# A trunk layer with retrieved experts: gathered rows issued in step with TensorE's tiles, and two one-hot buffers in the first half

## The reference, cut to what matters

```
act = gelu(einsum('nd,ned->ne', hx, expert_u[ix]))      # 128 picks of each token
return einsum('ne,ned->nd', act * gx, expert_v[ix])     # weighted sum of 128 rows of expert_v
```

## Time and profile before

| | us |
|---|---|
| median of 3 runs | 5171.36 (5170.26 to 5171.77) |
| the profiled execution, whole | 5173.29 |
| its span, first to last instruction | 5171.4 |

### The profile page before, as it was taken

One profiled execution on the slowest core, in us unless ns is written; L12 is line 12 of the kernel. 1 busy time (PEld: TensorE's weight loads), 2 busy tenths in 40 slices (PEclk: granted clock), 3 DMA queues, 4 the chain that ended last, 5 costly groups with the idle time before them and its releaser, 6 DMA issues.

```text
span 5171.4 us, 54598 instructions
## 1 busy us (share of the span) xinstructions
PE 4792.5 (93%) x22501; PEld 3572.5 (69%) x22501; DVE 3023.1 (58%) x4381; ACT 578.9 (11%) x1078; POOL 1701.1 (33%) x1113
## 2 busy tenths in 40 slices
PE   5989999998999999999999899999988899998869
PEld 1786446447998444466555346999988899997768
DVE  1441017886766765347777579666665517766671
ACT  1521001421222000000000011100000000000000
POOL 0131002663654655202544344223322203333220
PEclk7999999998999999999999999999999999999989
DMA  9919989993224989987999885688899959999994
GB/s 393 377 43 357 322 321 363 375 406 144 85 70 161 387 338 378 401 336 294 420 420 420 358 326 211 253 323 319 337 417 417 406 204 367 380 375 406 415 412 156
DMA packets 262299, 1666.66 MB, mean 322 GB/s; under 512 B 28274, under 2 KB 32770, under 8 KB 78660
## 3 DMA queue, kind: packets, MB, share of 16 engines
q0 software_dynamic: 130048, 939.72, 45.6%
q1 hardware_dynamic: 123460, 673.84, 33.9%
q10 hardware_dynamic: 8544, 49.62, 2.4%
HBM read 1643.31 MB, written 18.94 MB: 321 GB/s over the span
## 4 chain that ended last, share of the span: by engine, by line
PE 30%; DMA 18%; DVE 6%; issue 1%; POOL 0%; ACT 0%; ACTq 0%; DVEq 0%
PE ps L241 16%; DMA arena_sb<-peer_v 11%; PE ps L2289 8%; DMA arena_sb<-peer_u,arena_sb 6%; PE ps L1720 4%; PE ps L2232 2%; DVE arena_sb L400 1%; DVE arena_sb L395 1%; DMA arena_sb<-peer_v,arena_sb 1%; DVE arena_sb L2477 1%; POOL arena_sb L349 0%; DVE arena_sb L2002 0%; DVE arena_sb L2012 0%; DVE arena_sb L2004 0%; DVE arena_sb L1821 0%
## 5 line engine op out<-in xcount | busy, mean ns | idle before, releaser
L241 PE MATMUL ps<-arena_sb 128*128 128x224 f32 (+3 forms) x9728 | 2312.7, 399 | 5.0 <-PEq L552 2.4
L241 PEld LDWEIGHTS ps<-arena_sb 128*128 128x128 f32 x9728 | 1688.3, 193 | 623.4 <-issue 335.8
L400 DVE SCALAR_TENSOR_TENSOR arena_sb<-arena_sb 128x2048 f32<-128x2048 f32 x412 | 987.1, 2396 | 318.4 <-DMA arena_sb<-peer_v,arena_sb 301.4
L395 DVE CUSTOM_DVE_ANT_0 arena_sb<-arena_sb 128x2048 f32<-128x2048 f32 x416 | 961.7, 2332 | 222.3 <-DMA arena_sb<-peer_u,arena_sb 221.9
L349 POOL DMA_INDIRECT arena_sb<-peer_v,arena_sb x416 | 646.8, 1555 | 1071.0 <-DVE arena_sb L400 960.0
L2289 PE MATMUL ps<-arena_sb 128*128 128x224 f32 x4096 | 832.8, 364 | 141.2 <-DMA arena_sb<-peer_v 140.5
L349 POOL DMA_INDIRECT arena_sb<-peer_u,arena_sb x416 | 628.0, 1510 | 998.3 <-DVE arena_sb L395 792.4
L2289 PEld LDWEIGHTS ps<-arena_sb 128*128 128x128 f32 x4096 | 792.8, 196 | 179.7 <-DMA arena_sb<-peer_v 171.5
L1570 PE MATMUL ps<-arena_sb 128*128 128x512 f32 x768 | 342.2, 603 | 20.6 <-PEq L2594 7.4
L1720 PE MATMUL ps<-arena_sb 128*128 128x512 f32 x640 | 278.7, 598 | 17.0 <-DVE arena_sb L1501 13.5
L1570 PEld LDWEIGHTS ps<-arena_sb 128*128 128x128 f32 x768 | 145.8, 193 | 212.4 <-issue 194.9
(11 more groups left out here) (279 smaller groups left out, 2984.4 us busy)
## 6 DMA issues: line engine op xcount, KB each, us to landing
arena_sb<-peer_ut SPq DMA_DIRECT2D x128, 1024.0 KB, 8.3
arena_sb<-peer_v SPq DMA_DIRECT2D x128, 1024.0 KB, 15.3
arena_sb<-w_mod POOLq DMA_DIRECT2D x64, 1024.0 KB, 9.1
arena_sb<-w_qkv SPq DMA_DIRECT2D x48, 1024.0 KB, 8.7
arena_sb<-w_out SPq DMA_DIRECT2D x48, 1024.0 KB, 8.0
arena_sb<-w_query SPq DMA_DIRECT2D x48, 1024.0 KB, 6.9
arena_sb<-w_mod SPq DMA_DIRECT2D x32, 1024.0 KB, 8.9
arena_sb<-w_ga_r SPq DMA_DIRECT2D x32, 1024.0 KB, 7.7
```

The costliest lines, as they stand in the source:

```text
L241: mm = pe.matmul(out, weights[:, k * P:(k + 1) * P], x[:, k, :], start=(k == 0), stop=(k == chunks - 1))
L395: nc.vector.tensor_tensor_reduce(rows, rows, total, 1.0, 0.0, ALU.mult, ALU.add, seg.dots[:, p:p + 1]).then_inc(t.rows_used, 1)
L400: nc.vector.scalar_tensor_tensor(out=total, in0=rows, scalar=seg.weight[:, p:p + 1], in1=total, op0=ALU.mult, op1=ALU.add).then_inc(t.rows ...
```

## The change

`counts` is a new list of 253 entries, 375 rows in all. POOL goes through `behind` and, before it issues the rows of an entry k > 1 that has any, waits until `tile` is at least k - 1; the wait for the free slot stays. In h = 0 the one-hot operands get a second buffer, in memory that is otherwise used by `kept` from the V tiles on; group g uses buffer g % 2, `hot` of group g waits only for `gates` of group g - 2, and stands on DVE after the rows of tile s - 2 in place of s - 1 (groups 0 and 1 both after tile 11). In h = 1 there is one buffer and `hot` stands after the rows of tile s - 1, as before.

```
-    counts = ([0] * 10 + [2, 1] * 27 + [1, 2, 1, 2, 1, 1, 2, 1] * 8 + [2, 1] * 32 + [2] * 60)
+    counts = [0] * 8 + [2, 2, 2, 1] * 14 + [1, 2, 1, 1, 2] * 12 + [1, 2, 1, 1] + [2, 1, 2, 2] * 16 + [1] + [1, 2, 1, 1] * 15

     def _(pool):
-        gather_until(pool, nc, t, a, lead.stop)
-        pool.wait_ge(spare_in, 16 * 11)
-        gather_until(pool, nc, t, a, spare.stop)
-        pool.wait_ge(t.index_done, 1)
-        gather_until(pool, nc, t, a, last.stop)
+        for k, rows in enumerate(behind):
+            if k > 1 and len(rows):
+                pool.wait_ge(tile, k - 1)
+            for seg, known, n in ((spare, spare_in, 16 * 11), (last, t.index_done, 1)):
+                if seg.start in rows:
+                    gather_until(pool, nc, t, a, seg.start)
+                    pool.wait_ge(known, n)
+            gather_until(pool, nc, t, a, rows.stop)

-    weighted = ring[3][:, 0:TOKENS * P].rearrange("p (u n) -> p u n", u=TOKENS)
-    plain = ring[3][:, TOKENS * P:TOKENS * (P + HALF)].rearrange("p (u n) -> p u n", u=TOKENS)
+    hots = ring[3], t.m[:, C + 8192:C + 8192 + TILE]
+    weighted = [ap[:, 0:TOKENS * P].rearrange("p (u n) -> p u n", u=TOKENS) for ap in hots]
+    plain = [ap[:, TOKENS * P:TOKENS * (P + HALF)].rearrange("p (u n) -> p u n", u=TOKENS) for ap in hots]

+    hot_after = [{}, {s - 1: [g] for s, g in group_at[1].items()}]
+    for g, s in enumerate(starts[0]):
+        hot_after[0].setdefault(max(s - 2, starts[0][0] - 1), []).append(g)

         def hot(h, g):
-            n = GROUPS * h + g
-            if n:
+            n, i = GROUPS * h + g, 0 if h else g % 2
+            if h:
                 dve.wait_ge(gate_ps, n)
-            else:
+            elif n > 1:
+                dve.wait_ge(gate_ps, n - 1)
+            elif n == 0:

-                if s + 1 in group_at[h]:
-                    hot(h, group_at[h][s + 1])
+                for g in hot_after[h].get(s, ()):
+                    hot(h, g)
```

More of the change, by code:

```diff
@@ L2231, in gates @@
             for u in range(TOKENS):
-                mm = pe.matmul(t.ps[:, 2 + g % 2, u * HALF:(u + 1) * HALF], weighted[:, u], plain[:, u],
+                mm = pe.matmul(t.ps[:, 2 + g % 2, u * HALF:(u + 1) * HALF], weighted[i][:, u], plain[i][:, u],
                                start=True, stop=True)
@@ L2476, in hot @@
                 e = TOKENS * g + u
-                nc.vector.tensor_scalar(weighted[:, u], t.pick_iota, key1[:, e:e + 1], weight[:, e:e + 1],
+                nc.vector.tensor_scalar(weighted[i][:, u], t.pick_iota, key1[:, e:e + 1], weight[:, e:e + 1],
                                         ALU.is_equal, ALU.mult)
-            nc.vector.tensor_tensor(plain, over(t.pick_iota[:, HALF * h:HALF * (h + 1)], TOKENS),
+            nc.vector.tensor_tensor(plain[i], over(t.pick_iota[:, HALF * h:HALF * (h + 1)], TOKENS),
                                     wide(key0[:, TOKENS * g:TOKENS * (g + 1)], HALF),
```

## The result

The changed kernel takes 5044.6 us, median of 4 runs (5038.0 to 5049.2), against 5171.6 of the kernel before on the same chip: ratio 0.9753, 95% interval 0.9736 to 0.9770. That is 127 us less; the forecast was 157 less.

A forecast was written before the change was run, and what follows sets the result against it. PE was taken to be short of tiles while rows crowd the DMA engines, with DMA idling later while PE works. Terms -40 - 54 + 62 - 125 = -157 on 5171.4 gave 5014 us; 8 in 10 range 4950 to 5085.

The forecast's parts named there:

- Pacing in the V tiles: V tiles: POOL's wait for the tile limits rows per tile, gaining 54 us in h = 0 and 125 in h = 1.
- Two buffers and the earlier hot, h = 0: U tiles, h = 0: PE's 28 us of one-hot waits and the clock's 29 go; gain taken as 40 us.
- 15 us of the 55 for late rows: U tiles, h = 0: 15 of the 55 us lost there stay, because some late rows will show.
- DVE at 94%: U tiles, h = 0: DVE's work in seven tiles is 46.8 us against PE's 49.5, so it is nearly full.
- The new counts in U, h = 1: U tiles, h = 1: 14 two-row iterations delay hot, 33 us of waits plus 29 of clock, 62 us lost.
- Landing is no new limit: U tiles, h = 1: landing adds no cost, as seven rows in some 32 us is less than 4 in 14.
- rival L of e1: U, h = 1, rival in that run's own forecast: paced rows land late; part stays above 480 us, time above 5005.
- Rival A: U, h = 1: the clock holds, so only the 33 us of waits cost; 4985 us, chance 0.22.
- Costs of nothing: Last rows, segment finish, join(0) and rows starting at tile 8 cost nothing; kernel still runs 14 us beyond PE's end.
- B: V tiles: rows still get ahead of tiles, gains 24 and 75 in place of 54 and 125; 5094 us, chance 0.12.
- C: Both U parts: DVE binds through a closed loop, slower than before; 5248 at 2 us a tile more, chance 0.05.
- D: V tiles: pacing does nothing since slots hold the rows; V gains halved, 5103 us, chance 0.06.

The follow-up runs named there:

- e3: The changed kernel without POOL's wait for the tile, so rows are issued once a slot is free; 5134.6 us, ratio 0.9935 to the kernel before.
- e4: The kernel before with POOL's wait for the tile alone, old counts and one buffer; 5105.0 us, ratio 0.9863.
- e7: e6 with 9 rows moved from the V tiles of h = 0 to those of h = 1; 4970.0 us, ratio 0.9612.
- e8: e1 with the last stage's loads of x, gate row and norm cut to 64 of 2048 columns; 4950.5 us, ratio 0.9578.
- e6: e1 with the loads at the start of V, h = 1 spread over tiles and both segments' finish 4 tiles later; 4982.2 us, ratio 0.9626.
- e5: The kernel before with the second one-hot buffer and earlier one-hot work in h = 0 alone, old counts, no pacing; 5116.6 us, ratio 0.9897.
- e2: The changed kernel with rows in U, h = 1 counted 3, 1, 2, 1 in place of 2, 1, 2, 2; 4992.5 us, ratio 0.9652.
- e9: e1 with POOL's wait two tiles looser (k - 3 in place of k - 1), same rows per tile; 4974.8 us, ratio 0.9618.
- e1: The changed kernel with one-hot operands in h = 1 made after the rows of tile s - 2, not s - 1; 4979.2 us, ratio 0.9638.

## Why the prediction was right, by its steps

**Pacing in the V tiles: right, both sizes a little too high.** The mechanism is shown by e3 and e4 for h = 0. V, h = 0 gained 47.5 of 54: a tile took 404.6 / 64 = 6.3 us where I took 6.2. I had set 2.52 MB against the 413 GB/s of the earlier trace rows and taken 6.2 us, 406 GB/s; the part ran at 401 with a share of 1.01, which is 6.28 us. e7 shows that the row count holds this part: with 9 rows fewer it took 10 us less, and PE hardly waits. That 401 GB/s is all that DMA gives for this mix is not shown: e8, with the same counts there, ran at 406. V, h = 1 gained 103.7 of 125, of which 57 come from the smaller count alone and 47 from the pacing on top of it (e3; with the old counts the pacing alone gains only 24 there, e4); the forecast gave the wait for the tile the whole. There I put 10 us for four loads of 4.2 MB at 413 GB/s (they are 3.4 MB, since the second block of x has 32 rows); the mis-sized term is the loads. The rest of x, 2.9 MB, and two stores of y come in the same part, and each MB of the loads costs 2.7 us (e8), 16.7 us in all. Spreading them saved nothing (e6). 64 tiles at 6.15 are 394; e8 without these loads, but with the stores and the 32 identity matmuls, took 405.6.

**Two buffers and the earlier hot, h = 0: right.** I kept 15 us of the 55 for late rows. e5 gives back 54, with the old counts, and e2, e3, e8 and e9 give back 53 to 54 with the new ones (441.5 to 442.0). The changed kernel, e1, e6 and e7 are 5 us longer, and the difference is one wait: PE's weight loads wait 2.4 to 2.9 us for the first group's one-hot operand there (2.9 at 3329.97 in the changed kernel), and the clock falls once after it; in the other four no such wait is over 1.8 us. DVE at 94%, which I feared, did not show in PE's time otherwise, although DVE did wait 31.6 us for `peer_v` rows.

**The new counts in U, h = 1: right in place and kind, too small in size.** I forecast 14 waits, 33 us, and 29 us of clock, 62 together; the part grew by 79. The 14 waits came as forecast, 32.6 us. Two terms were off.

The first is the clock. It is 0.92 over the 456 us from 4140 on, 16% of the time at 1.2 instead of 2.4 GHz, 73 us, of which half, 36, is lost: 2.6 us for each of the 14 waits, where I had taken 29 / 14 = 2.1 from h = 0. That division was wrong. Of the 14 waits of the earlier trace rows only 11 are over 2 us (2.2 to 2.5); the other three are 0.5 to 0.7 us, and the clock around them is 1.00 (windows 3436 to 3452, 3550 to 3570 and 3663 to 3680 us of the kernel before). 29 / 11 is 2.6, the price found here. The chain shows where it goes: after the wait at 4309 the gate matmuls are 1.75 us longer and the next two tiles 1.8.

The second is a wait that I had put at nothing ("Landing is no new limit"): 8.1 us ahead of the first group's gates, and a clock of 0.92 over the first 64 us, some 5 us more. Paced rows land just before they are used there, DVE runs late, and the first one-hot work with it. Without the pacing this wait is absent and the part 10.7 us shorter (e3). 33 + 36 + 8 + 5 is 82, near the 79 measured. So rival L of e1 holds for one wait of 15.

Rival A (the clock holds), to which I gave 0.22, is out. What I did not see when I had priced the stall was that it was free to remove: one iteration earlier, the single buffer is already free, and e1's median is 65 us lower with a change of one character.

**Costs of nothing: right.** From the end of the last V tile to the end of the span it is 14.0 us in both kernels; the last segment's finish stayed hidden.

**Rivals.** B (rows still ahead of the tiles) may have a part in the 6 and 21 us that the V parts fell short, but a small one in h = 0, where PE's waits for `peer_v` are at most 1.7 us. The pieces of 2 KB that it names do not by themselves leave PE short: before, such tiles took 11.1 us against 7.3 for pieces of 4 KB, but with more rows running free beside them, and with paced rows they keep PE busy (4830 to 4880 us: 50.0 of 50). C (DVE binds both U parts) did not occur; its loop shows only in the wait of 8.1 us. D is out by e3.

**The best kernel.** e1, e2, e6, e7 and e9 all beat both kernels; their intervals (0.959 to 0.968) overlap, so no one of them is shown to be the best. The step that counts is e1's.

## What to carry to other kernels

When two streams share DMA, let the one with slack be issued by the progress of the engine that the other one feeds, and choose its count per step with the waits of that engine in view, not from the highest rate seen. Before adding work to an engine that runs in program order, look for what stands behind it in the same iteration and who waits for that; moving the awaited piece ahead by one iteration was worth 65 us, half of what the whole change brought, and needed no memory. A repeated wait of PE of 2.1 to 2.6 us cost about twice its length here, since the clock fell after it; in the kernel before, the three waits under 0.75 us had no such price, nor did the 53 for `peer_v` in h = 0, about 1 us each and 2.2 at most, where the clock is 1.00.

## What the runs showed of the hardware that was not expected

A DMA busy share near 1.00 goes with no one rate, and does not say that PE is short of data. At a share of 0.99 to 1.02 the core moved 417 GB/s with 26 gathered rows and 14 tiles in 100 us (before, V of h = 0), 412 with U tiles and rows (e1), 401 with paced rows and V tiles, and 386 with the same tiles and fewer rows (e7). Here are 100 us of the third kind, 100 us of the first, and then the whole of V, h = 0, in e7:

```profile
3900.00:4000.00 100.00, 96.63 (x506) 94.85 (x505) 51.45 (x45) 0.00 (x0) 32.36 (x22) 1.00 1.00 400
```

```profile
3880.00:3980.00 100.00, 86.63 (x440) 81.78 (x439) 59.81 (x52) 2.86 (x8) 24.53 (x26) 1.00 1.02 417
```

```profile
3688.00:4083.00 395.00, 390.47 (x2049) 386.43 (x2050) 187.73 (x141) 5.58 (x16) 101.37 (x81) 1.00 0.99 386
```

In the last of these PE waits 3.8 us for tiles, and in e1's U tiles it is busy for 446 of 448 us: there the rate is what was asked for, not a limit. In the changed kernel, where V tiles are loaded in pieces of 2 KB and PE is busy throughout (4830 to 4880 us), it is 374 GB/s at 0.99. How much of these differences is a limit of the mix (the size of the pieces is one candidate, the turns between queues another) was not tested on its own.
